# A decoder layer on one core: first-stage expert gathers split in two, four more picks in that stage, three pair buffers in the second

## The chip, the cores and the metric

The kernel runs on one core of a Trainium2 chip. The metric is the device time of one execution in microseconds (us). Engines: PE (TensorE, matmul), DVE (VectorE), ACT (ScalarE), POOL (GpSimd), SP (SyncE, which here only issues DMAs).

## What is computed

One layer of a decoder: attention and a spatial gating unit beside each other, then PEER (retrieval over 128 x 128 experts, each with one row of `u` and one of `v`), then a gated projection and a norm. 512 tokens, width 2048, float32. The change is all in PEER:

```
def peer(a, w_q, k1, k2, u_exp, v_exp):
    q = (a @ w_q).reshape(B, S, PEER_HEADS, PEER_QDIM)
    ...
    top, sel = lax.top_k(cand, PEER_TOPK)
    experts = jnp.take_along_axis(cand_idx, sel, axis=-1)
    gates = jax.nn.softmax(top, axis=-1)
    ...
        u_sel = jnp.take(u_exp, e_c, axis=0)
        h = jnp.einsum('bthkd,btd->bthk', u_sel, a_c, preferred_element_type=jnp.float32)
        w = (g_c * jax.nn.gelu(h)).astype(a_c.dtype)
        v_sel = jnp.take(v_exp, e_c, axis=0)
        return jnp.einsum('bthk,bthkd->btd', w, v_sel)
```

With 8 heads and 16 experts each, every token has 128 experts.

## The kernel before, in words

**Two ways for PEER.** For the first 344 tokens (`TD`) the kernel works densely: it multiplies with all 16384 rows of `u`, weighs the results with a sparse matrix of gates, and multiplies with all rows of `v`. For the last 128 tokens and 40 more it gathers the rows of the chosen experts. A *pick* is one gather of a `u` row and a `v` row for each of the 128 partitions: 128 picks for the last 128 tokens and 43 (`B_PICKS`, `idx_b`) for the 40 tokens, 171 in all (`PICKS`).

**The first stage** (here also: u stage) streams `peer_u` in 128 chunks, one PE slot each: `tile()` makes 16 x 3 = 48 matmuls of 344 columns (each product as three: high x high, high x low, low x high). The first 32 chunks lie between the routing steps of the heads; from chunk 36 to 118 the picks are spread over the slots. For each slot, SP loads 1 MB (`raw`), ACT rounds it (`wH`, line 656), DVE takes the rest (`wL`, line 1110), one slot ahead of PE. DVE scales the finished chunk (`scale_chunk`, 1534), ACT applies the gelu and stores it into `pair` in HBM.

**The second stage** (v stage) streams `peer_v` in 128 slots of 48 matmuls. Each slot also readies one chunk of `pair` for later: SP loads pre-activations and gates together (`pair_in`, 348 KB, `load_chunk`, 435), POOL multiplies them (`apply_gates`, 609), ACT rounds (`weight_hi`, 912) and DVE takes the rest (`weight_lo`, 1644). Eight chunks make a group, for which PE waits.

**A pick** has these steps. POOL issues the gather. DVE makes the dot product (`dot`, 1604, line 1617). ACT makes the gelu and the weight (`weigh_pick`, 923). DVE adds the weighed `v` row (`add_row`, 1619, line 1629 or 1634). The order of DVE's work is written out by hand: step `o` stands for the dot (even) or the add (odd) of pick `o // 2`, and `u_step(c)` and `v_step(g, q)` say between which slots the steps stand:

```
    return (min(max(c, FIRST_PICK), LAST_PICK) - FIRST_PICK) * 2 * (U_PICKS - LATE) // (LAST_PICK - FIRST_PICK)
```

`U_PICKS` picks belong to the first stage, `LATE` = 4 of them to its last 8 slots; the others to the second. `FIRST_PICK` is 36, `LAST_PICK` 118. In a slot DVE does: scale the last chunk, one step, `wL` for the next slot, another step where there is one. It waits in this order, so a late row holds up `wL`.

**POOL's queue** is also written by hand. The sparse matrix of gates is built by indirect DMAs that add one column of 128 gates into `pair` (`add_gates`, line 565): 384 in all, the first 156 before the first pick (`ADDS_FIRST`), the others four after each gather (614 to 619). A gather of the first stage (`gather`, 583) fetches rows of 16 KB, `u` and `v` side by side (`uv_rows`), into one of three buffers (`rows`), and waits until the pick that had the buffer is added (`pick_done`). In the second stage `gather_u` (597) and `gather_v` (605) fetch rows of 8 KB apart; the first waits for the dot of the buffer's last pick alone.

Of the kernel before, what the change touches and what calls it, by code (L numbers as in the profile page):

```python
# [27 lines left out]
HEADS = 8  # L28
# [4 lines left out]
TOPK = 16  # L33
KEYS = 128
# [18 lines left out]
FIRST_PICK, LAST_PICK = ROUTE_U + 4, KEYS - GROUP - 2  # L53
U_PICKS, LATE = 64, 4
TAIL = 6
# [120 lines left out]
def trunk_layer(nc, a, stream, out, pair_dram):  # L176
# [8 lines left out]
    def at(name, shape, dt, offset):  # L185
        return nc.alloc_sbuf_tensor_at(name, [P] + shape, dt, offset=base + offset)
# [114 lines left out]
    with ctx:  # L301
        ps = ctx.enter_context(nc.psum_tensor("ps", [P, 8, 512], F))

        def sem(name):
            return ctx.enter_context(nc.semaphore(name))
# [29 lines left out]
        pre_stored = [sem(f"pre_stored{i}") for i in range(2)]  # L335
        pair_loaded = [sem(f"pair_loaded{i}") for i in range(2)]
        g_scaled = sem("g_scaled")
# [10 lines left out]
        row_landed = [sem(f"row_landed{i}") for i in range(6)]  # L348
        v_row_landed = [sem(f"v_row_landed{i}") for i in range(3)]
        dot_done, dot_gelu, pick_weighed, pick_done = sem("dot_done"), sem("dot_gelu"), sem("pick_weighed"), sem("pick_done")  # L350
# [41 lines left out]
        def _(sp):  # L392
# [41 lines left out]

            def load_chunk(c, b):

                if isinstance(c, int):
                    sp.wait_ge(pre_stored[b], (c - b) * 8 + 16)
                if not (isinstance(c, int) and c < 2):
                    sp.wait_ge(act_wlo, c - 1)  # L440
                sp.dma_start(pair_in[b][:, :], pair_rows[:, c, 0:PW + TD]).then_inc(pair_loaded[b], 16)

            for c in range(KEYS - GROUP, KEYS):
                load(nu + c, stream["pu"][c, :, :], c % 2)
                if c == KEYS - GROUP:
# [3 lines left out]
                load_chunk(c - KEYS + GROUP, c % 2)  # L449

# [6 lines left out]
            def load_late_chunk(v):  # L457

                if v == GROUP:
                    for b in range(2):  # L460
                        sp.wait_ge(pre_stored[b], 8 * KEYS)
                load_chunk(GROUP + v, v % 2)

# [34 lines left out]
        def _(pool):  # L498
# [102 lines left out]
            def gather_v(j):  # L601

                if ROW_USED[j] >= 0:
                    pool.wait_ge(pick_done, ROW_USED[j] + 1)
                pool.indirect_dma_start(  # L605
                    out=rows[ROW_AT[j]][:, 1, :], out_offset=None, in_=a["v_rows"],
                    in_offset=bass.IndirectOffsetOnAxis(ap=ids_of(j), axis=0)).then_inc(v_row_landed[ROW_AT[j] - 3], 16)

            def apply_gates(c, b):

                pool.wait_ge(pair_loaded[b], (c - b) * 8 + 16)
                nc.gpsimd.tensor_tensor(pre_in[b], pre_in[b], gate_in[b], ALU.mult).then_inc(act_gated, 1)  # L612

            for j in range(U_PICKS - LATE + 1):
                gather(j)
                if j >= 1:
                    for n in range(added, min(added + 4, HEADS * NTD * TOPK)):
                        add_gates(n)
                        added = n + 1
            assert added == HEADS * NTD * TOPK  # L620
            for c in range(GROUP):
                apply_gates(c, c % 2)
                if c % 2 == 0 and U_PICKS - LATE + 1 + c // 2 < U_PICKS:
                    gather(U_PICKS - LATE + 1 + c // 2)
            for j in range(U_PICKS, U_PICKS + 2):
                gather_u(j)
                gather_v(j)
            for g in range(NGROUPS - 1):
                for q in range(GROUP):
                    apply_gates(GROUP * (g + 1) + q, q % 2)  # L630
# [12 lines left out]
        def _(act):  # L643
# [348 lines left out]
            def v_beat(g, q, b, m, i, tail=False):  # L992
# [3 lines left out]
                if isinstance(g, int) and (g, q) == (0, 0):  # L996
# [101 lines left out]
        def _(dve):  # L1098
# [554 lines left out]
            for c in range(ROUTE_U + 2, KEYS):  # L1653
# [654 lines left out]
```

## Time and profile before

| | us |
|---|---|
| median of 3 runs | 2978.49 (2977.01 to 2980.55) |
| the profiled execution's own time | 2979.05 |
| its span in the trace | 2977.3 |
| PE busy | 2923.9 |
| DVE busy | 2259.8 |
| ACT busy | 1268.4 |
| POOL busy | 1440.4 |

An engine's busy time is the union of its instructions; neighbouring matmuls overlap in it, so that a short stop of PE shows less idle time than it costs. On POOL an indirect DMA counts as busy for as long as POOL writes its descriptors; the transfer goes on after that.

### The profile page before, as it was taken

The numbers are of one execution on the slowest core, as the hardware profiler recorded it, in microseconds if no ns is written. First come the engines' busy times: TensorE is split into PE (matmuls) and PEld (weight loads), VectorE is DVE, ScalarE is ACT, GpSimd is POOL, SyncE is SP. The second block draws the span as 40 slices with busy tenths as digits, with TensorE's granted clock in tenths as the row PEclk, the third lists the DMA queues.
The fourth block names the chain that finished last, engine by engine and source line by source line (L and its number), as shares of the span: only waits on it lengthen the run. The fifth ranks groups of instructions, "written<-read, shape, count | busy, mean of one in ns | idle before, by whom it ended". The sixth has DMA issues, their size and how long they took to land.

```text
span 2977.3 us, 43219 instructions
## 1 busy us (share of the span) xinstructions
PE 2923.9 (98%) x16888; PEld 2739.3 (92%) x16888; DVE 2259.8 (76%) x2836; ACT 1268.4 (43%) x1898; POOL 1440.4 (48%) x859
## 2 busy tenths in 40 slices
PE   9999999999999999999999999999999999999998
PEld 7888668889999999999999999999999999999787
DVE  5466664578888877877787769888888889998545
ACT  5224541333333433333333344555555555566522
POOL 1012000008888778888888235443445778772000
PEclk9999999999999999999999999999999999999999
DMA  8469422235555599999999889999999999998222
GB/s 299 169 238 331 142 85 99 99 110 128 139 125 130 140 343 358 373 361 358 372 341 361 320 350 408 411 417 418 415 417 415 417 413 416 417 395 314 92 93 98
DMA packets 195807, 843.09 MB, mean 283 GB/s; under 512 B 66780, under 2 KB 87276, under 8 KB 116556
## 3 DMA queue, kind: packets, MB, share of 16 engines
q0 software_dynamic: 104592, 413.77, 37.9%
q1 hardware_dynamic: 72336, 404.83, 36.0%
q10 hardware_dynamic: 18732, 22.59, 2.2%
q8 instruction: 85, 1.39, 0.2%
q14 instruction: 62, 0.51, 0.0%
HBM read 768.01 MB, written 73.06 MB: 282 GB/s over the span
## 4 chain that ended last, share of the span: by engine, by line
PE 66%; DVE 13%; DMA 11%; POOL 5%; issue 3%; ACT 2%; SPq 0%; DVEq 0%; ACTq 0%; POOLq 0%
PE ps L1838 21%; PE ps L1836 21%; PE ps L1837 21%; DMA pair_in<-pair 7%; DVE wL L1110 4%; DVE rows L1617 3%; POOL pair_in L612 2%; DVE hT L1629 2%; POOL rows L597 1%; POOL rows L605 1%; DMA rows<-u_rows,idx_s 1%; DVE b_acc L1634 1%; ACT wH L656 1%; DMA rows<-v_rows,idx_b 1%; DMA raw<-s_v 1%
## 5 line engine op out<-in xcount | busy, mean ns | idle before, releaser
L1836 PE MATMUL ps<-aH,wH 128*128 128x344 f32 (+2 forms) x3088 | 1057.4, 342 | 6.3 <-DVE wL L1110 6.3
L1838 PE MATMUL ps<-aH,wL 128*128 128x344 f32 (+2 forms) x3088 | 1055.4, 342 | 0.0
L1837 PE MATMUL ps<-aL,wH 128*128 128x344 f32 (+2 forms) x3088 | 1047.1, 339 | 0.0
L565 POOL DMA_INDIRECT pair<-gates_r,idx_d x384 | 740.5, 1928 | 376.7 <-DVE gates_r L1525 242.5
L1110 DVE TENSOR_TENSOR wL<-raw,wH 128x2048 fp32r<-128x2048 f32 x333 | 778.1, 2337 | 183.2 <-ACT wH L656 180.8
L656 ACT ACTIVATE wH<-raw 128x2048 fp32r<-128x2048 f32 x333 | 636.3, 1911 | 591.5 <-PE ps L1838 538.6
L1836 PE MATMUL ps<-actH,wH 128*128 128x344 f32 x2048 | 656.7, 321 | 14.3 <-DVE wL L1110 13.8
L1838 PE MATMUL ps<-actH,wL 128*128 128x344 f32 x2048 | 656.1, 320 | 0.0
L1837 PE MATMUL ps<-actL,wH 128*128 128x344 f32 x2048 | 651.6, 318 | 0.0
L1836 PEld LDWEIGHTS ps<-aH,wH 128*128 128x128 f32 x3088 | 578.5, 187 | 47.1 <-DVE wL L1110 5.8
L1837 PEld LDWEIGHTS ps<-aL,wH 128*128 128x128 f32 x3088 | 580.6, 188 | 38.8 <-issue 1.0
L1838 PEld LDWEIGHTS ps<-aH,wL 128*128 128x128 f32 x3088 | 579.9, 188 | 38.2
L1836 PEld LDWEIGHTS ps<-actH,wH 128*128 128x128 f32 x2048 | 383.7, 187 | 21.9 <-DVE wL L1110 20.9
L1837 PEld LDWEIGHTS ps<-actL,wH 128*128 128x128 f32 x2048 | 384.9, 188 | 0.0
L1838 PEld LDWEIGHTS ps<-actH,wL 128*128 128x128 f32 x2048 | 384.1, 188 | 0.0
L612 POOL TENSOR_TENSOR pair_in<-pair_in 128x344 f32<-128x344 f32 x128 | 194.2, 1518 | 316.2 <-DMA pair_in<-pair 315.6
L1629 DVE SCALAR_TENSOR_TENSOR hT<-rows,pick_w,hT 128x2048 f32<-128x2048 f32 x128 | 305.6, 2387 | 5.4 <-issue 2.1
L1617 DVE SCALAR_TENSOR_TENSOR rows<-rows,ps 128x2048 f32<-128x2048 f32 x128 | 291.8, 2280 | 6.7 <-DMA rows<-uv_rows,idx_s 5.5
L1534 DVE TENSOR_TENSOR ut<-ps,rstd 128x344 f32<-128x344 f32 x128 | 66.0, 516 | 154.4 <-PE ps L1838 135.5
L597 POOL DMA_INDIRECT rows<-u_rows,idx_s x64 | 109.6, 1713 | 70.9 <-DVE rows L1617 48.0
L931 ACT ACTIVATE dots<-dots 128x1 f32<-128x1 f32 x128 | 25.7, 201 | 271.9 <-DVE rows L1617 262.2
L1646 DVE TENSOR_TENSOR actL<-pair_in,actH 128x344 fp32r<-128x344 f32 x128 | 67.2, 525 | 95.4 <-ACT actH L914 85.9
(288 smaller groups left out, 2626.7 us busy)
## 6 DMA issues: line engine op xcount, KB each, us to landing
raw<-s_pu SPq DMA_DIRECT2D x128, 1024.0 KB
raw<-s_pv SPq DMA_DIRECT2D x128, 1024.0 KB
pair<-zeros POOLq DMA_DIRECT2D x44, 1024.0 KB, 8.7
pair_in<-pair SPq DMA_DIRECT2D x128, 348.0 KB
pair<-ut ACTq DMA_DIRECT2D x128, 172.0 KB
raw<-s_out SPq DMA_DIRECT2D x16, 1024.0 KB
raw<-s_pq SPq DMA_DIRECT2D x16, 1024.0 KB
raw<-s_gate SPq DMA_DIRECT2D x16, 1024.0 KB
```

What stands on the lines that cost most here:

```text
L565: pool.indirect_dma_start(out=gates_flat, out_offset=bass.IndirectOffsetOnAxis(ap=idx_d[0:m, t, c:c + 1], axis=0), in_=gates_r[0:m, t, c:c ...
L597: pool.indirect_dma_start(out=rows[ROW_AT[j]][:, 0, :], out_offset=None, in_=a["u_rows"], in_offset=bass.IndirectOffsetOnAxis(ap=ids_of(j) ...
L612: nc.gpsimd.tensor_tensor(pre_in[b], pre_in[b], gate_in[b], ALU.mult).then_inc(act_gated, 1)
L656: A(wH[parity][:, :], raw[at_n][:, :], ACT.Copy).then_inc(hi_ready, 1)
L1110: V.tensor_tensor(wL[parity][:, :], src[:, :], wH[parity][:, :].bitcast(F), ALU.subtract).then_inc(lo_ready, 1)
L1534: V.tensor_tensor(ut[b][:, :], ps[:, 6 + b, 0:TD], rstd[:, 0:TD], ALU.mult).then_inc(chunk_scaled, 1)
L1617: V.scalar_tensor_tensor(r3, r3, 1.0, act_of, ALU.mult, ALU.mult, accum_out=d).then_inc(dot_done, 1)
L1629: V.scalar_tensor_tensor(hT[:, :, TA:T], v3, pick_w[:, i:i + 1], hT[:, :, TA:T], ALU.mult, ALU.add).then_inc(pick_done, 1)
L1646: V.tensor_tensor(actL[b][:, j, 0:TD], src, actH[b][:, j, 0:TD].bitcast(F), ALU.subtract).then_inc(act_wlo, 1)
L1836: mm(out, wh, xh, start=start, stop=False, skip_group_check=skip_group_check)
L1837: mm(out, wh, xl, start=False, stop=False, skip_group_check=skip_group_check)
L1838: return mm(out, wl, xh, start=False, stop=stop, skip_group_check=skip_group_check)
```

## The change

1. Each gather of the first stage becomes a `gather_u` and a `gather_v` with rows of 8 KB, with semaphores of their own; of the four `add_gates` of a pick, two stand behind each. `gather` and the array `uv_rows` go.
2. `U_PICKS` is 68 instead of 64: four picks move from the second stage into the first.
3. `pair_in` has three buffers in the second stage (chunk `c` from 8 on uses buffer `(c - 8) % 3`); a load waits for the chunk that last used its buffer, and stands one slot earlier in SP's queue.
4. In a slot of the second stage ACT rounds the chunk (`weight_hi`) before it weighs a pick instead of after.

```diff
-U_PICKS, LATE = 64, 4
+U_PICKS, LATE = 68, 4
...
+def pair_at(c):
+
+    return c % 2 if c < GROUP else (c - GROUP) % 3
...
-    pair_in = [at(f"pair_in{i}", [PW + TD], F, C0 + 4 * KB * i) for i in range(2)]
+    pair_in = [at(f"pair_in{i}", [PW + TD], F, C0 + o) for i, o in enumerate((0, 4 * KB, 7 * KB))]
...
-            def load_chunk(c, b):
-
-                if isinstance(c, int):
-                    sp.wait_ge(pre_stored[b], (c - b) * 8 + 16)
-                if not (isinstance(c, int) and c < 2):
-                    sp.wait_ge(act_wlo, c - 1)
+            def load_chunk(c):
+
+                b = pair_at(c)
+                sp.wait_ge(pre_stored[c % 2], (c - c % 2) * 8 + 16)
...
+                if PAIR_PREV[c] >= 0:
+                    sp.wait_ge(act_wlo, PAIR_PREV[c] + 1)
...
+            load_late_chunk(3)
             for v in range(3, KEYS - GROUP):
-                load_late_chunk(v)
+                if v + 1 < KEYS - GROUP:
+                    load_late_chunk(v + 1)
...
-            def gather(j):
-
-                if ROW_USED[j] >= 0:
-                    pool.wait_ge(pick_done, ROW_USED[j] + 1)
-                pool.indirect_dma_start(
-                    out=rows[ROW_AT[j]][:, :, :].rearrange("p a d -> p (a d)"), out_offset=None, in_=a["uv_rows"],
-                    in_offset=bass.IndirectOffsetOnAxis(ap=ids_of(j), axis=0)).then_inc(row_landed[ROW_AT[j]], 16)
...
             for j in range(U_PICKS - LATE + 1):
-                gather(j)
+                gather_u(j)
                 if j >= 1:
-                    for n in range(added, min(added + 4, HEADS * NTD * TOPK)):
+                    for n in range(added, min(added + 2, HEADS * NTD * TOPK)):
+                        add_gates(n)
+                        added = n + 1
+                gather_v(j)
+                if j >= 1:
+                    for n in range(added, min(added + 2, HEADS * NTD * TOPK)):
                         add_gates(n)
                         added = n + 1
...
                 if not tail:
+                    c = GROUP * (g + 1) + q
+                    weight_hi(c, q, 1 - b, pre_in[pair_at(c)])
                     for o in range(v_step(g, q), v_step(g, q + 1)):
                         if o % 2 == 0:
                             weigh_pick(o // 2)
-                    weight_hi(GROUP * (g + 1) + q, q, 1 - b, pre_in[q % 2])
...
-                if j >= U_PICKS:
-                    dve.wait_ge(v_row_landed[ROW_AT[j] - 3], 16 * ROW_TURN[j])
+                dve.wait_ge(v_row_landed[ROW_AT[j]], 16 * ROW_TURN[j])
```

The order of POOL's instructions where the picks of the first stage begin (`pair` from `gates_r` is an added column of gates, `rows` a gather; the text behind a row says what it waits for). Before:

```order
L583 DMA rows_86<-uv_rows,idx_s 128x4096 [waits a_tok_ready]
L583 DMA rows_87<-uv_rows,idx_s 128x4096
L565 DMA pair<-gates_r,idx_d 11534336x1 x4
L583 DMA rows_88<-uv_rows,idx_s 128x4096
L565 DMA pair<-gates_r,idx_d 11534336x1 x4
L583 DMA rows_86<-uv_rows,idx_s 128x4096 [waits pick_done]
```

And in the changed kernel, from the same place:

```order
L602 DMA rows_86<-u_rows,idx_s 128x2048 [waits a_tok_ready]
L610 DMA rows_86<-v_rows,idx_s 128x2048
L602 DMA rows_87<-u_rows,idx_s 128x2048
L578 DMA pair<-gates_r,idx_d 11534336x1 x2
L610 DMA rows_87<-v_rows,idx_s 128x2048
L578 DMA pair<-gates_r,idx_d 11534336x1 x2
L602 DMA rows_88<-u_rows,idx_s 128x2048
L578 DMA pair<-gates_r,idx_d 11534336x1 x2
```

Where POOL had one gather and four adds for a pick, it has two gathers and four adds.

ACT's order in a slot of the second stage (`actH` from `pair_in` is `weight_hi`, `dots` and `pick_w` are `weigh_pick`). Before:

```order
L656 ACTIVATE wH_71<-raw_67 128x2048 [waits tile_done,raw_loaded0]
L983 ACTIVATE hT<-ps 128x344 [waits h_acc,tile_done]
L973 ACTIVATE ps<-hT 128x344 [waits h_acc]
L931 ACTIVATE dots<-dots 128x1 [waits dot_done]
L935 ACTIVATE pick_w<-dots,gates_r 128x1 [waits dot_gelu]
L914 ACTIVATE actH_82<-pair_in_138 128x344 [waits act_gated]
```

And in the changed kernel:

```order
L668 ACTIVATE wH_71<-raw_67 128x2048 [waits tile_done,raw_loaded0]
L995 ACTIVATE hT<-ps 128x344 [waits h_acc,tile_done]
L985 ACTIVATE ps<-hT 128x344 [waits h_acc]
L926 ACTIVATE actH_82<-pair_in_139 128x344 [waits act_gated]
L943 ACTIVATE dots<-dots 128x1 [waits dot_done]
L947 ACTIVATE pick_w<-dots,gates_r 128x1 [waits dot_gelu]
```

The chunk's rounding stands ahead of the pick's gelu, and the buffers go round by three (137, 138, 139).

## Rows read from the trace of the kernel before

**Rows 1.** The page: span, busy time by engine, granted PE clock in 40 slices

```profile
span 2977.3 us, 43219 instructions
...
PE 2923.9 (98%) x16888; PEld 2739.3 (92%) x16888; DVE 2259.8 (76%) x2836; ACT 1268.4 (43%) x1898; POOL 1440.4 (48%) x859
PEclk9999999999999999999999999999999999999999
```

**Rows 2.** Windows of the first stage's picks and of the second stage: busy of each engine

```profile
core 0: us, PE busy (x) PEld busy (x) DVE busy (x) ACT busy (x) POOL busy (x), PEclk, DMA share, GB/s
1065.90:1761.00 695.10, 694.33 (x4401) 694.04 (x4401) 539.30 (x383) 245.08 (x320) 511.65 (x294) 1.00 0.98 355
1761.00:2754.00 993.00, 978.68 (x6177) 970.72 (x6176) 877.38 (x610) 552.30 (x977) 556.12 (x334) 1.00 1.00 406
```

**Rows 3.** Windows of 100 us inside the first and inside the second stage

```profile
1200.00:1300.00 100.00, 100.00 (x636) 100.00 (x635) 79.01 (x58) 35.27 (x47) 84.21 (x49) 1.00 1.00 360
2300.00:2400.00 100.00, 98.51 (x624) 98.09 (x623) 89.32 (x60) 56.64 (x100) 71.72 (x35) 1.00 1.02 417
```

**Rows 4.** Groups by line on POOL, 1100 to 1650 us: xcount | busy us, mean ns | idle before

```profile
L565 POOL DMA_INDIRECT pair<-gates_r,idx_d x210 | 393.3, 1873 | 73.1 <-issue 63.4 <-DMA pair<-gates_r,idx_d 9.7
L583 POOL DMA_INDIRECT rows<-uv_rows,idx_s x53 | 67.7, 1277 | 18.0 <-issue 15.5 <-DVE hT L1629 2.5
```

**Rows 5.** Timeline of POOL at the first pick and at the last adds of gates

```profile
1052.55 1.00 POOL L583 DMA_INDIRECT rows<-uv_rows,idx_s  x1 [13.09 <-DVE ps L1600]
...
1649.63 1.42 POOL L565 DMA_INDIRECT pair<-gates_r,idx_d  x1 [0.30 <-issue]
1651.36 2.51 POOL L565 DMA_INDIRECT pair<-gates_r,idx_d  x1 [0.30 <-issue]
1654.17 1.96 POOL L565 DMA_INDIRECT pair<-gates_r,idx_d  x1 [0.30 <-issue]
1656.43 0.99 POOL L583 DMA_INDIRECT rows<-uv_rows,idx_s  x1 [0.30 <-issue]
1657.73 0.97 POOL L583 DMA_INDIRECT rows<-uv_rows,idx_s  x1 [0.30 <-issue]
1685.33 0.94 POOL L583 DMA_INDIRECT rows<-uv_rows,idx_s  x1 [26.63 <-DVE hT L1629]
```

**Rows 6.** Waits of DVE for rows of picks, 1040 to 1770 us

```profile
DVE rows L1617 <- DMA rows<-uv_rows,idx_s: 5.5, 5, 1.8
```

**Rows 7.** Timeline of POOL and of DVE where an add of gates took long

```profile
1321.03 1.54 POOL L565 DMA_INDIRECT pair<-gates_r,idx_d  x1 [0.30 <-issue]
1322.87 3.24 POOL L565 DMA_INDIRECT pair<-gates_r,idx_d  x1 [0.30 <-issue]
...
1322.35 2.34 DVE L1629 SCALAR_TENSOR_TENSOR hT<-rows,pick_w,hT 128x2048 f32<-128x2048 f32 x1
1324.61 2.29 DVE L1110 TENSOR_TENSOR wL<-raw,wH 128x2048 fp32r<-128x2048 f32 x1
1326.82 2.28 DVE L1617 SCALAR_TENSOR_TENSOR rows<-rows,ps 128x2048 f32<-128x2048 f32 x1
```

**Rows 8.** Groups by line on POOL, 1770 to 2300 us, then 2300 to 2700 us

```profile
L605 POOL DMA_INDIRECT rows<-v_rows,idx_s x56 | 63.1, 1127 | 24.2 <-DVE hT L1629 14.2 <-issue 6.2
...
L605 POOL DMA_INDIRECT rows<-v_rows,idx_b x42 | 102.2, 2433 | 12.4 <-issue 7.5 <-DVE b_acc L1634 3.4
L597 POOL DMA_INDIRECT rows<-u_rows,idx_b x42 | 84.3, 2007 | 12.4 <-DVE rows L1617 4.9 <-issue 4.6
```

**Rows 9.** First matmul of each product in the second stage, 1761 to 2754 us

```profile
L1836 PE MATMUL ps<-actH,wH 128*128 128x344 f32 x2048 | 656.7, 321 | 14.3 <-DVE wL L1110 13.8
```

**Rows 10.** Waits for chunks, 1850 to 2300 us, then 2300 to 2700 us

```profile
POOL pair_in L612 <- DMA pair_in<-pair: 217.0, 53, 6.3
...
ACT actH L914 <- POOL pair_in L612: 70.6, 22, 4.1
...
POOL pair_in L612 <- DMA pair_in<-pair: 68.3, 30, 5.1
ACT actH L914 <- POOL pair_in L612: 64.7, 31, 4.1
```

More of the change, by code:

```diff
@@ L133, in raw_at @@
     return (v - 2) % 4 if 4 <= v < KEYS - GROUP else n % 2
+def pair_at(c):
+    return c % 2 if c < GROUP else (c - GROUP) % 3
+PAIR_PREV, PAIR_LANDED = [], []
+for _c in range(KEYS):
+    _same = [j for j in range(_c) if pair_at(j) == pair_at(_c)]
+    PAIR_PREV.append(_same[-1] if _same else -1)
+    PAIR_LANDED.append(16 * (1 + len(_same)))
 RAW_PREV, RAW_LANDED = [], []
@@ L335, in trunk_layer @@
         pre_stored = [sem(f"pre_stored{i}") for i in range(2)]
-        pair_loaded = [sem(f"pair_loaded{i}") for i in range(2)]
+        pair_loaded = [sem(f"pair_loaded{i}") for i in range(3)]
         g_scaled = sem("g_scaled")
@@ L348, in trunk_layer @@
         row_landed = [sem(f"row_landed{i}") for i in range(6)]
-        v_row_landed = [sem(f"v_row_landed{i}") for i in range(3)]
+        v_row_landed = [sem(f"v_row_landed{i}") for i in range(6)]
         dot_done, dot_gelu, pick_weighed, pick_done = sem("dot_done"), sem("dot_gelu"), sem("pick_weighed"), sem("pick_done")
@@ L433, in _ @@
             pair_rows = pair_dram.rearrange("(p c) s t -> p c (s t)", c=KEYS)
-            def load_chunk(c, b):
-                if isinstance(c, int):
-                    sp.wait_ge(pre_stored[b], (c - b) * 8 + 16)
-                if not (isinstance(c, int) and c < 2):
-                    sp.wait_ge(act_wlo, c - 1)
+            def load_chunk(c):
+                b = pair_at(c)
+                sp.wait_ge(pre_stored[c % 2], (c - c % 2) * 8 + 16)
+                if b == 2 and PAIR_PREV[c] < 0:
+                    for i in range(2):
+                        sp.wait_ge(pre_stored[i], 8 * KEYS)
+                if PAIR_PREV[c] >= 0:
+                    sp.wait_ge(act_wlo, PAIR_PREV[c] + 1)
                 sp.dma_start(pair_in[b][:, :], pair_rows[:, c, 0:PW + TD]).then_inc(pair_loaded[b], 16)
@@ L448, in _ @@
                     sp.wait_ge(b_loaded, 32 * SETS)
-                load_chunk(c - KEYS + GROUP, c % 2)
+                load_chunk(c - KEYS + GROUP)
             def load_value(v):
@@ L457, in load_late_chunk @@
             def load_late_chunk(v):
[L459 to L462, printed above, removed]
+                load_chunk(GROUP + v)
             for v in range(3):
@@ L606, in gather_v, with apply_gates @@
                     out=rows[ROW_AT[j]][:, 1, :], out_offset=None, in_=a["v_rows"],
-                    in_offset=bass.IndirectOffsetOnAxis(ap=ids_of(j), axis=0)).then_inc(v_row_landed[ROW_AT[j] - 3], 16)
-            def apply_gates(c, b):
-                pool.wait_ge(pair_loaded[b], (c - b) * 8 + 16)
+                    in_offset=bass.IndirectOffsetOnAxis(ap=ids_of(j), axis=0)).then_inc(v_row_landed[ROW_AT[j]], 16)
+            def apply_gates(c):
+                b = pair_at(c)
+                pool.wait_ge(pair_loaded[b], PAIR_LANDED[c])
                 nc.gpsimd.tensor_tensor(pre_in[b], pre_in[b], gate_in[b], ALU.mult).then_inc(act_gated, 1)
             for j in range(U_PICKS - LATE + 1):
-                gather(j)
+                gather_u(j)
                 if j >= 1:
-                    for n in range(added, min(added + 4, HEADS * NTD * TOPK)):
+                    for n in range(added, min(added + 2, HEADS * NTD * TOPK)):
[4 more added lines that the diff above has]
+                    for n in range(added, min(added + 2, HEADS * NTD * TOPK)):
                         add_gates(n)
@@ L621, in _ @@
             for c in range(GROUP):
-                apply_gates(c, c % 2)
+                apply_gates(c)
                 if c % 2 == 0 and U_PICKS - LATE + 1 + c // 2 < U_PICKS:
-                    gather(U_PICKS - LATE + 1 + c // 2)
+                    gather_u(U_PICKS - LATE + 1 + c // 2)
+                    gather_v(U_PICKS - LATE + 1 + c // 2)
             for j in range(U_PICKS, U_PICKS + 2):
@@ L629, in _ @@
                 for q in range(GROUP):
-                    apply_gates(GROUP * (g + 1) + q, q % 2)
+                    apply_gates(GROUP * (g + 1) + q)
                     for o in range(v_step(g, q), v_step(g, q + 1)):
@@ L959, in _ @@
                 u_beat(c, c % 2, nu + c, 0)
-                weight_hi(c - KEYS + GROUP, c - KEYS + GROUP, 0, pre_in[c % 2])
+                weight_hi(c - KEYS + GROUP, c - KEYS + GROUP, 0, pre_in[pair_at(c - KEYS + GROUP)])
                 for o in range(u_step(c), u_step(c + 1)):
@@ L1662, in _ @@
                 if c >= KEYS - GROUP:
-                    weight_lo(c - KEYS + GROUP, c - KEYS + GROUP, 0, pre_in[c % 2])
+                    weight_lo(c - KEYS + GROUP, c - KEYS + GROUP, 0, pre_in[pair_at(c - KEYS + GROUP)])
                 if late_dot:
@@ L1679, in v_end @@
                     accumulate(2 * q, CUM[m + q - 1] + 4 * GROUP * i + 1)
-                weight_lo(c, q, 1 - b, pre_in[q % 2])
+                weight_lo(c, q, 1 - b, pre_in[pair_at(c)])
             scale_chunk(KEYS - 1, 1, CUM[nu + KEYS - 1])
@@ L2276 @@
         "s_pv": v["peer_v"][0].reshape(KEYS, NGROUPS, GROUP, GROUP, WIDE).transpose(1, 3, 0, 2, 4).reshape(KEYS, P, 2048),
-        "uv_rows": np.concatenate([v["peer_u"][0], v["peer_v"][0]], axis=1),
         "u_rows": v["peer_u"][0],
```

## The prediction

> **What bounds the kernel now.** I read the page first: of a span of 2977.3 us PE is busy 2923.9, at full clock (the level of 2.4 GHz) throughout [rows 1]. So nothing that the change does can save more than PE's stops in the stages it touches, and it costs what it makes PE wait.
>
> The windows give those stops [rows 2]. In the first stage's stretch PE starts 4401 matmuls in 695.1 us, 0.1579 us each, and is idle under 1 us: there is nothing to win there. In the second stage it starts 6177 in 993.0 us; at 0.1579 each that is 975.6, so 17.4 us is all that better supply could give. The group of PE's first matmuls agrees: 14.3 us idle, 13.8 of them behind `wL` of DVE [rows 9].
>
> Next comes what stands close behind PE in the first stage. DVE is busy 79% in a window of 100 us there [rows 3]. POOL is the one to look at: its groups from 1100 to 1650 us show 393.3 us of adds of gates and 67.7 us of gathers, and 91.1 us of "idle" [rows 4]. Of that idle, 78.9 us are the 0.3 us between two of its instructions ("issue"), 9.7 us are waits for its own adds, and only 2.5 us are waits for a free buffer. In 550 us POOL stands free for 2.5. It ends its last add at 1656 us and first waits for something long (26.63 us) at 1685 [rows 5]. DVE already waited five times for a row, 5.5 us in all [rows 6]. POOL's queue is thus as full as PE's.
>
> **The cadence.** A slot is 48 matmuls, 48 x 100/636 = 7.55 us [rows 3]. `u_step` lays 60 picks over 82 slots: one each 82/60 x 7.55 = 10.32 us. POOL needs for one pick four adds and a gather, 4 x (1.873 + 0.30) + (1.277 + 0.30) = 8.69 + 1.58 = 10.27 us [rows 4]. They just match.
>
> **First edit, gathers in two.** The order of POOL shows one more indirect DMA for every pick, as the diff says. No row shows the time of an 8 KB gather among the adds; the nearest are gathers of 16 KB there, 1.277 us in the mean and 0.94 to 1.00 at the shortest [rows 4, 5], and those of 8 KB in the second stage, 1.127 us in its earlier part and 2.0 to 2.4 in its later [rows 8]. Half the bytes are not half the time: POOL pays for issuing. I take 1.277 + 0.30 = 1.58, so POOL now needs 11.85 us for a pick.
>
> **Second edit, four more picks.** 64 picks over the same 82 slots: one each 82/64 x 7.55 = 9.67 us. The deficit is 11.85 - 9.67 = 2.18 us for a pick. It lasts while there are adds to do: 384 - 156 = 228, four at each pick, 57 picks. 57 x 2.18 = 124 us. DVE's order is fixed, so a late row holds `wL` of the next slot, and PE, which has no idle time in this stage, gives all of it to the end. POOL's head start is none, since its buffers were hardly ever full.
>
> Two things make it less. POOL's instruction is held while DVE runs certain of its own: an add that took 3.24 us instead of 1.54 began at 1322.87, and ended some 1.4 us after `add_row` (1322.35 + 2.34) had [rows 7]. The mean of 1.873 has 0.33 of this over 1.54, the gather's 1.277 some 0.28 over 1.00. With PE and DVE slowed to POOL's pace, `add_row` and `wL` fill 5.3 us of 11.85 instead of 5.5 of 10.32 (2.34 + 1.28 or 1.37 x 2.29), so I shrink the excess by 16%: 0.05 for each of 6 instructions, 0.3 a pick, 17 us. And a first transfer of 1 MB lands earlier than one of 2 MB, by 1.05 MB at 360 GB/s, 2.9 us, once. That leaves 104; between 124 and 104 I take **+110 us**.
>
> The Trainium skill (SBUF — State Buffer, section "A bandwidth-pool intuition that's wrong") says that GpSimd cannot write a DMA's descriptors until DVE releases the port that they share, and gives 3100 ns in place of 620 for such a case. The row of 3.24 us agrees in kind; if every added gather cost that page's 3.1 us instead of 1.58, the deficit would be 87 us larger.
>
> Ends of this term: were every instruction as short as an undisturbed one, 4 x (1.54 + 0.30) + 2 x (1.00 + 0.30) = 9.96 us, 0.29 x 57 = +17 us [rows 5, 7]. Were both gathers as the slowest group, 2.43 + 0.30 [rows 8], 2 x 1.15 x 57 = 131 more, +241. The mean of 53 gathers under the same DVE is nearer than either.
>
> After pick 57 POOL has no adds and catches up in a few us; pick 57 now stands in slot 109, and the chunks' loads, which wait for all adds, in slot 120, eleven slots or 83 us later, so I cost the rest of the stage at nothing. Its cover is POOL's and SP's idle time there, of which the wait of 26.63 us is an instance [rows 5].
>
> **Second stage.** 103 picks instead of 107 stand in it: DVE is freed of 4 x (2.28 + 2.34) = 18 us of 877 [rows 2, 7], and 8.4 MB less are moved, 20 us at 417 GB/s [rows 3] in a stage whose DMA share is 1.00 [rows 2]. The third buffer and the earlier load act on POOL's waits for chunks, 217.0 and 68.3 us, and so on ACT's, 70.6 and 64.7 [rows 10]. All this only reaches PE through `wL`, so the gain lies between 0 and 17.4 us. With `weight_hi` first, a late chunk now holds a pick's weight and with it `add_row` and `wL`; what that could cost no row tells, and I bound it by the stage's present stops once more, 14.3 us. I take **-12 us**: fewer steps hit PE's own cause, a `wL` behind a step.
>
> **Sum.** 2979.05 (profiled execution) + 110 - 12 = 3077.1. The median of the runs lies 0.56 lower, at 2978.49, so 3076.5 us.
>
> **Rivals.**
> - *POOL fits after all* (faster). If the changed phase of its work against DVE's spares it the collisions, it needs by its shortest rows 4 x (1.42 + 0.30) + 2 x (0.94 + 0.30) = 9.36 us [rows 5]. The point is 9.67 us a pick; under it the first stage stays as it is and the second gives 12: 2966.5. Against it: the mean of 210 adds is 1.873, and even at 1.54 each it fails. Chance 0.07.
> - *The transfers bind, not POOL.* The first stage has a DMA share of 1.00 at 360 GB/s [rows 3]. If that is its limit and POOL's time gives way, 8.4 MB more cost 23 us there: 2978.5 + 23 - 12 = 2989.5. Against it: PE lost nothing in it so far, the second stage moves 417 GB/s at the same share, and the adds' length goes with DVE's instructions. Chance 0.05. The Trainium skill (DMA: Bandwidth & Descriptors, "Specifications") puts HBM's limit for a core at about 358 GB/s, which is this rival's rule; the second stage's 417 disagrees with it.
> - *Collisions grow.* POOL, now always late, falls into step with DVE as in the later second stage, and both gathers cost 2.73: 3076.5 + 131 = 3207.5. For it: [rows 8]. Against: there POOL has 8 KB gathers in a different order of DVE's work. Chance 0.05.
> - *Nothing to be seen*, by half of the first: 0.03.
>
> **Numbers.** The forecast has 0.80. The range leaves out the rivals at 2966.5, 2989.5 and 3207.5 and the outer parts of the forecast's own. Its low end goes two thirds of the way from +110 to +17, which is +48, with all of the 17.4 won: 3009. Its high end goes half of the way from +110 to +241, +175, with nothing won: 3154. About 0.2% is what a measurement of this kernel can tell from no change. Faster by more: 0.07; within: 0.03; slower: 0.90.
>
> **What would show it.** Right: the last add near 1656 + 91 + what it waits, about 1740 us; DVE's dots waiting for rows some 50 times, near 90 us in all, where it was 5.5; PE idle behind `wL` by near 100 us between 1100 and 1750; the stretch from the first pick to the second stage about 805 us instead of 695; POOL without any wait for a buffer in it; a second stage of about 981 us. Wrong: adds at 1.55 us and a first stage as long as before; or a first stage longer while POOL shows waits (then it is the transfers); or a second stage over 993 us.

## The result, and the profile after

| | before | changed |
|---|---|---|
| median, us | 2979.52 (4 runs) | 3100.95 (3099.46 to 3103.39, 4 runs) |
| the profiled execution's span, us | 2977.3 | 3097.7 |

The ratio is 1.0399 (95% interval 1.0381 to 1.0418): slower by 121 us.

The page of the changed kernel, against [rows 1]; of part 2 the slices of PE, of POOL and of the granted PE clock:

```profile
span 3097.7 us, 43283 instructions
...
PE 2962.5 (96%) x16888; PEld 2774.5 (90%) x16888; DVE 2315.2 (75%) x2836; ACT 1272.8 (41%) x1898; POOL 1497.7 (48%) x923
...
PE   9999999999999998888798899999999999999998
...
POOL 1012000028888688888888823544444666663000
PEclk9999999999999999989998999999999999999999
...
PE 68%; POOL 18%; DVE 5%; issue 5%; DMA 3%; ACT 1%; SPq 0%; ACTq 0%; DVEq 0%; POOLq 0%
```

The same rows of the kernel before that [rows 1] leaves out:

```profile
PE   9999999999999999999999999999999999999998
...
PE 66%; DVE 13%; DMA 11%; POOL 5%; issue 3%; ACT 2%; SPq 0%; DVEq 0%; ACTq 0%; POOLq 0%
```

The loss stands in one place. PE, with a 9 in every slice of the middle before, has 8s and a 7 from the 16th on; the granted clock, full before, has two 8s. And in the chain of what ended last (the last row, each engine's share of it) POOL's part rose from 5 to 18%, while those of DVE and of the DMAs fell.

The windows of the two stages and of 100 us in each, against [rows 2, 3]:

```profile
1065.90:1897.00 831.10, 736.16 (x4406) 726.18 (x4405) 558.55 (x395) 248.25 (x328) 629.03 (x365) 0.94 0.90 308
1897.00:2874.40 977.40, 973.57 (x6178) 972.24 (x6176) 914.36 (x598) 553.09 (x969) 500.26 (x326) 1.00 0.99 404
...
1200.00:1300.00 100.00, 79.44 (x469) 77.73 (x467) 61.23 (x44) 26.54 (x35) 85.68 (x48) 0.94 0.88 289
2300.00:2400.00 100.00, 100.00 (x636) 100.00 (x635) 91.55 (x57) 54.98 (x96) 44.93 (x33) 1.00 1.01 415
```

The first stage's stretch takes 831.1 us instead of 695.1 for the same matmuls (4401 and 4406 of them recorded), the second 977.4 instead of 993.0. +136.0 and -15.6: that is the whole difference of the spans, 120.4 us. In the window of 100 us in the first stage DVE fell from 79 to 61% and the DMA share from 1.00 to 0.88, while POOL went from 84 to 86%. Of the three, POOL alone had no time to lose.

In the changed kernel's lines, 578 is `add_gates`, 602 `gather_u`, 610 `gather_v`, 618 `apply_gates`, 1630 the dot, 1641 and 1646 `add_row`, 1123 `wL`, 1848 to 1850 the matmuls. POOL's groups, 1100 to 1700 us (columns as in [rows 4]), and then its timeline at the last adds of gates:

```profile
L578 POOL DMA_INDIRECT pair<-gates_r,idx_d x195 | 382.7, 1962 | 65.4 <-issue 59.2 <-DMA pair<-gates_r,idx_d 6.2
L602 POOL DMA_INDIRECT rows<-u_rows,idx_s x48 | 70.2, 1463 | 14.6 <-issue 13.1 <-DVE rows L1630 1.5
L610 POOL DMA_INDIRECT rows<-v_rows,idx_s x49 | 56.6, 1155 | 14.9 <-issue 14.9
```

```profile
1760.51 1.45 POOL L578 DMA_INDIRECT pair<-gates_r,idx_d  x1 [0.30 <-issue]
1762.27 1.42 POOL L578 DMA_INDIRECT pair<-gates_r,idx_d  x1 [0.31 <-issue]
1764.00 0.99 POOL L602 DMA_INDIRECT rows<-u_rows,idx_s  x1 [0.30 <-issue]
```

POOL's idle time is "issue", 0.3 us each, 6.2 us of waits for its own adds, and 1.5 us of waits for a buffer. An add takes 1.962 us (it was 1.873), the two gathers 1.463 and 1.155 us. So a pick costs POOL 4 x 2.262 + 1.763 + 1.455 = 12.27 us. The last add ends at 1763.7 us instead of 1656.1.

Who waits for it, 1040 to 1900 us (before: [rows 6], and the last line here, from 1040 to 1770 us of the kernel before):

```profile
DVE rows L1630 <- DMA rows<-u_rows,idx_s: 110.2, 33, 5.5
DVE hT L1641 <- issue: 97.5, 32, 5.6
...
DVE hT L1641 <- DMA rows<-v_rows,idx_s: 6.6, 3, 2.8
...
PE ps L1848 <- DVE wL L1123: 94.9, 34, 6.1
...
PE ps L1836 <- DVE wL L1110: 0.8, 1, 0.8
```

DVE waits 33 times for a `u` row and 32 times before an add of a `v` row ("issue" is a wait whose releaser the profile does not name; it stands at the same instruction as the three waits for `v_rows`). PE then waits 94.9 us behind `wL`, which stands behind those steps in DVE's order. That is less than the 136 us by which the stage grew; the rest is time in which PE ran at the lower clock (last section).

In the second stage, PE's first matmuls (against [rows 9]) and waits from 1990 to 2440 us (against [rows 10]):

```profile
L1848 PE MATMUL ps<-actH,wH 128*128 128x344 f32 x2048 | 656.5, 321 | 3.8 <-DVE wL L1123 3.8
...
POOL rows L610 <- DVE hT L1641: 129.9, 43, 5.0
...
POOL pair_in L618 <- DMA pair_in<-pair: 9.9, 7, 2.9
```

PE's idle time fell from 14.3 to 3.8 us. POOL waited 217.0 us for chunks in the stretch shown before; now it waits for buffers of picks instead.

### The profile page after: what moved, and what is told of

It reads as the page before. It is cut to its first block, busy times and chain, and to the rows that moved or that the text cites. A ratio compares the mean times of both kernels' runs of the same rounds, so it can differ in the third digit from the quotient of the medians.

```text
span 3097.7 us, 43283 instructions
## 1 busy us (share of the span) xinstructions
PE 2962.5 (96%) x16888; PEld 2774.5 (90%) x16888; DVE 2315.2 (75%) x2836; ACT 1272.8 (41%) x1898; POOL 1497.7 (48%) x923
## 3 DMA queue, kind: packets, MB, share of 16 engines
q8 instruction: 85, 1.39, 0.2%
## 4 chain that ended last, share of the span: by engine, by line
PE 68%; POOL 18%; DVE 5%; issue 5%; DMA 3%; ACT 1%; SPq 0%; ACTq 0%; DVEq 0%; POOLq 0%
PE ps L1850 22%; PE ps L1848 22%; PE ps L1849 22%; POOL pair L578 13%; POOL rows L602 2%; POOL rows L610 2%; DVE wL L1123 1%; DMA rows<-u_rows,idx_s 1%; DVE hT L1641 1%; DMA rows<-v_rows,idx_s 1%; ACT wH L668 1%; PE ps L2046 1%; DVE rows L1630 1%; PE ps L2102 0%; PE ps L2023 0%
## 5 line engine op out<-in xcount | busy, mean ns | idle before, releaser
L1848 PE MATMUL ps<-aH,wH 128*128 128x344 f32 (+2 forms) x3088 | 1076.8, 349 | 100.5 <-DVE wL L1123 100.5
L1849 PE MATMUL ps<-aL,wH 128*128 128x344 f32 (+2 forms) x3088 | 1065.2, 345 | 0.0
L1848 PEld LDWEIGHTS ps<-aH,wH 128*128 128x128 f32 x3088 | 593.3, 192 | 151.2 <-DVE wL L1123 109.6
L1849 PEld LDWEIGHTS ps<-aL,wH 128*128 128x128 f32 x3088 | 594.8, 193 | 38.5 <-issue 1.0
L1850 PEld LDWEIGHTS ps<-aH,wL 128*128 128x128 f32 x3088 | 593.5, 192 | 38.3
L1641 DVE SCALAR_TENSOR_TENSOR hT<-rows,pick_w,hT 128x2048 f32<-128x2048 f32 x128 | 330.2, 2580 | 110.0 <-issue 99.1
L1630 DVE SCALAR_TENSOR_TENSOR rows<-rows,ps 128x2048 f32<-128x2048 f32 x128 | 291.9, 2281 | 112.7 <-DMA rows<-u_rows,idx_s 110.2
L602 POOL DMA_INDIRECT rows<-u_rows,idx_s x128 | 178.9, 1398 | 234.0 <-DVE rows L1630 188.7
L610 POOL DMA_INDIRECT rows<-v_rows,idx_s x128 | 185.8, 1452 | 192.7 <-DVE hT L1641 170.9
L618 POOL TENSOR_TENSOR pair_in<-pair_in 128x344 f32<-128x344 f32 x128 | 150.7, 1178 | 44.1 <-DMA pair_in<-pair 41.7
L1646 DVE SCALAR_TENSOR_TENSOR b_acc<-rows,pick_wb,b_acc 128x2048 f32<-128x2048 f32 x42 | 132.6, 3156 | 2.7 <-ACT pick_wb L947 1.7
```

What stands on the lines that cost most here:

```text
L602: pool.indirect_dma_start(out=rows[ROW_AT[j]][:, 0, :], out_offset=None, in_=a["u_rows"], in_offset=bass.IndirectOffsetOnAxis(ap=ids_of(j) ...
L610: pool.indirect_dma_start(out=rows[ROW_AT[j]][:, 1, :], out_offset=None, in_=a["v_rows"], in_offset=bass.IndirectOffsetOnAxis(ap=ids_of(j) ...
L1630: V.scalar_tensor_tensor(r3, r3, 1.0, act_of, ALU.mult, ALU.mult, accum_out=d).then_inc(dot_done, 1)
L1641: V.scalar_tensor_tensor(hT[:, :, TA:T], v3, pick_w[:, i:i + 1], hT[:, :, TA:T], ALU.mult, ALU.add).then_inc(pick_done, 1)
L1646: V.scalar_tensor_tensor(b_acc[:, :, :], v3, pick_wb[:, i:i + 1], b_acc[:, :, :], ALU.mult, ALU.add).then_inc(pick_done, 1)
L1848: mm(out, wh, xh, start=start, stop=False, skip_group_check=skip_group_check)
```

## The experiments

Each kernel ran beside the kernel before on the same chip, where that one's median was 2981.8 to 2982.5 us; the ratios are to those runs. "Stage 1 end" is the start of the first matmul of the second stage in the PE timeline: 1761.0 us before, 1897.1 in the changed kernel. "Stage 2" is from there to the end of its last matmul: 993.0 and 977.3 us. Each is from one profile. Kernels whose second stage is the same differ in it by 1 to 2 us (before and `split_only`; `picks_only` and `picks_aligned`), and the first pick began up to 4.3 us later than before (`picks_only`), so differences of that size say nothing.

### The two halves of the first stage's edit, apart

`split_only` is the kernel before with the two gathers of 8 KB and the adds two and two (its two main lines):

```diff
-                gather(j)
+                gather_u(j)
...
+                gather_v(j)
```

> The kernel before with one edit: gathers of the first stage as two of 8 KB rows, adds two and two; 64 picks there, second stage as it was. POOL's queue (my theory): POOL needs per pick four adds and two gathers, 12.27 us by the changed kernel's profile (4 x 2.26 + 1.76 + 1.46), against 10.32 us between picks; 57 x 1.95 = 111 us, so about 3090 us, with adds of gates back to back and DVE waiting for rows. Transfers bind (rival): not a byte is added, so about 2980 us. Half and half between splitting and the added picks (a second rival, that the loss is of the four more picks alone): about 2980 us too.

Measured: 3089.79 us, ratio 1.0352 (1.0328 to 1.0376). Last add 1769.3 us, stage 1 end 1872.4, stage 2 995.0. Not one byte was added, and 111.4 of the 136 us are there, as POOL's queue gives it. The rival that the added picks do it alone is gone.

`picks_only` is the kernel before with `U_PICKS` 68:

```diff
-U_PICKS, LATE = 64, 4
+U_PICKS, LATE = 68, 4
```

> The kernel before with one edit: 68 instead of 64 picks in the first stage, gathers of 16 KB kept. POOL's queue: 10.27 us of POOL for a pick against 9.67 between picks, 57 x 0.6 = 34 us in the first stage, less some 8 us that four picks fewer give in the second: about 3005 us. Transfers bind: 8.4 MB more at 360 GB/s in the first stage, 23 us, less 8: about 2994 us, and then POOL would show waits for buffers; by POOL's queue it shows none.

Measured: 3015.64 us, ratio 1.011 (1.0088 to 1.0131). Last add 1668.7, stage 1 end 1811.4 (+50.4), stage 2 980.0 (-13.0). Both theories were too low. The last add comes only 12.6 us later than before, but the picks now stand earlier: pick 57 in slot 109 instead of 114, 5 x 7.55 = 38 us. 12.6 + 38 = 51, the lengthening measured. Of the 12.6 us, 4.3 were there at the first gather (1056.9 instead of 1052.6 us); for the rest, the 228 adds took 1.94 us in the mean instead of 1.89.

The two halves make 111.4 + 50.4 = 161.8 us, more than the 136.1 of both together: the 4.3 us are in it, and in each half alone the adds grew (by 0.09 and 0.05 us) as much as or nearly as much as in the kernel with both (0.07). The rest of the difference is not accounted for.

### Is it POOL's time or the transfers?

`short_v` is the changed kernel with 2 KB of each first-stage `v` row instead of 8:

```diff
-                    out=rows[ROW_AT[j]][:, 1, :], out_offset=None, in_=a["v_rows"],
+                    out=rows[ROW_AT[j]][:, 1, 0:D // 4] if short else rows[ROW_AT[j]][:, 1, :], out_offset=None,
+                    in_=a["v_short"] if short else a["v_rows"],
```

> The changed kernel, but from pick 3 on the v row of a first-stage pick is fetched with 2 KB instead of 8 KB; the rest of the row stays as an earlier pick left it, so this part of the sum is left out. POOL issues the same instructions, the transfers of a pick shrink from 2.1 MB to 1.3 MB. POOL's queue: nothing moves, about 3098 us, first stage about 830 us from 1066. Transfers bind: 65 x 0.79 MB less at 360 GB/s, 142 us less: about 2965 us.

Measured: 3101.61 us, ratio 1.0396 (1.0367 to 1.0426); last add 1764.3, stage 1 end 1899.4. POOL's groups from 1100 to 1700 us and the window 1200 to 1300:

```profile
L578 POOL DMA_INDIRECT pair<-gates_r,idx_d x194 | 375.6, 1936 | 65.0 <-issue 58.5 <-DMA pair<-gates_r,idx_d 6.4
L602 POOL DMA_INDIRECT rows<-u_rows,idx_s x48 | 81.0, 1687 | 14.6 <-issue 14.3 <-DVE rows L1632 0.3
L611 POOL DMA_INDIRECT rows<-v_short,idx_s x49 | 51.1, 1044 | 14.9 <-issue 14.9
...
1200.00:1300.00 100.00, 85.04 (x488) 83.61 (x489) 64.67 (x47) 27.43 (x38) 85.07 (x50) 0.91 0.77 230
```

230 GB/s instead of 289, a DMA share of 0.77 instead of 0.88, and the time is the changed kernel's. The bytes do not bind. The rows also say what POOL pays for: 1.044 us for a gather of 2 KB rows, 1.155 for one of 8 KB, 1.277 for one of 16 KB [rows 4], all of them means that hold some collisions with DVE.

This leaves the number of transfers, which `short_v` keeps. In the changed kernel, at the 33 dots for which DVE waited, the dot began 4.6 to 7.8 us after POOL's gather instruction had ended, 6.6 us in the mean of the earlier half and 6.7 in that of the later. Had the transfers piled up behind POOL, this time would have grown.

`no_adds` takes POOL's other work away (one place of the edit is shown; the kernel leaves 228 columns of gates out of the result):

```diff
-                if j >= 1:
-                    for n in range(added, min(added + 2, HEADS * NTD * TOPK)):
-                        add_gates(n)
-                        added = n + 1
                 gather_v(j)
```

> The changed kernel without the 228 adds of gates that stand among the picks (three quarters of the sparse gates of five heads are left out). Gathers of 8 KB and 68 picks stay. POOL's queue: a pick costs POOL 3.3 us against 9.67, the first stage is back at 695 us, total about 2960 us. Were it DVE or the added transfers that 68 picks overload, some of the 136 us would stay, at least the 23 us of the added bytes or DVE waiting for rows.

Measured: 2964.29 us, ratio 0.9931 (0.9904 to 0.9958). The windows of its two stages:

```profile
1066.00:1761.70 695.70, 695.70 (x4411) 695.70 (x4410) 558.33 (x395) 246.68 (x328) 277.91 (x138) 1.00 0.94 368
1761.70:2739.00 977.30, 973.28 (x6178) 971.46 (x6176) 915.06 (x598) 553.09 (x969) 501.24 (x326) 1.00 0.99 403
```

The first stage is at 695.7 us, PE without any idle time, POOL at 40%. DVE with 68 picks and the transfers with 368 GB/s have room. The run takes away the adds' small transfers along with POOL's time for them; that these did not hold the rows up is the reading just before.

### Can the four picks be had without the loss?

`joined_spread` is the changed kernel with gathers of 16 KB again and the 228 adds spread over 64 picks:

```diff
-                    for n in range(added, min(added + 2, HEADS * NTD * TOPK)):
...
+                    for n in range(added, ADDS_FIRST + (HEADS * NTD * TOPK - ADDS_FIRST) * j // (U_PICKS - LATE)):
```

> The changed kernel with gathers of 16 KB again and the 228 adds of gates spread over all 64 picks of the loop (3 or 4 at each) instead of four at each of 57; 68 picks, three pair buffers and the new rounding order kept. POOL's queue: 3.56 x 2.17 + 1.58 = 9.3 us for a pick against 9.67 between picks, so the first stage is back at about 696 us and the second keeps its 977: about 2963 us, faster than both kernels. Transfers bind: the first stage still has 8.4 MB more, 23 us: about 2986 us.

Measured: 2988.77 us, ratio 1.0014 (0.9998 to 1.0029). Stage 1 end 1787.3, 26.3 us too long; stage 2 976.5. The total is near the transfers' 2986, but `short_v` speaks against that theory, and the expectation from POOL's queue missed by 26 us. POOL's timeline at the first border between two heads, and all such waits:

```profile
1157.64 0.99 POOL L596 DMA_INDIRECT rows<-uv_rows,idx_s  x1 [0.30 <-issue]
1158.93 1.45 POOL L578 DMA_INDIRECT pair<-gates_r,idx_d  x1 [0.30 <-issue]
1172.13 1.55 POOL L578 DMA_INDIRECT pair<-gates_r,idx_d  x1 [11.74 <-DMA pair<-gates_r,idx_d]
...
POOL pair L578 <- DMA pair<-gates_r,idx_d: 37.2, 4, 11.7
```

The first add of a head waits until the adds of the head before have landed (the kernel says so in `add_gates`). Here the last of those was issued right behind a gather of 2 MB, and POOL stood 11.74 us; before, a gather lay between that add and the wait, and the longest wait was 3.6 us.

`joined_aligned` lets a head's adds end with a pick:

```diff
+            def adds_by(j):
+
+                ends = [(0, 156), (10, 192), (23, 240), (37, 288), (50, 336), (64, 384)]
+                for (j0, n0), (j1, n1) in zip(ends, ends[1:]):
+                    if j <= j1:
+                        return n0 + (n1 - n0) * (j - j0) // (j1 - j0)
```

> As joined_spread, but the adds of a head now end with a pick, so that the next head's first add, which waits for them, stands behind one more gather. In joined_spread those four waits cost POOL 37.2 us (up to 11.7 each), because the last add had just been issued behind a gather; before they cost 3.2 each. If that is the cause of its first stage being 26 us longer, the waits fall to about 13 us, the first stage to within 5 us of 695 and the whole to about 2966 us. If it is POOL's mean load (3.6 adds and a gather, 9.4 to 9.7 us against 9.67), 2985 us stays.

Measured: 2969.71 us, ratio 0.9962 (0.9949 to 0.9975). Its stages, and POOL's waits from 1050 to 1720 us:

```profile
1066.00:1761.20 695.20, 694.32 (x4401) 694.04 (x4400) 556.76 (x395) 246.73 (x328) 512.25 (x298) 1.00 0.99 367
1761.20:2738.80 977.60, 973.99 (x6178) 972.55 (x6176) 917.25 (x598) 552.99 (x969) 502.12 (x326) 1.00 1.00 404
...
POOL rows L596 <- DVE hT L1651: 48.2, 13, 16.7
...
POOL pair L578 <- DMA pair<-gates_r,idx_d: 11.6, 4, 4.6
```

The four waits cost 11.6 us, POOL has 48.2 us of slack (waits for a buffer), the first stage is at 695.2 and the second at 977.6 us. This kernel is faster than both, than the kernel before by 0.4%.

`split_aligned` has the same spread with gathers of 8 KB, two adds behind the `u` row and the rest behind the `v` row:

```diff
-                    for n in range(added, min(added + 2, HEADS * NTD * TOPK)):
+                    for n in range(added, min(added + 2, adds_by(j))):
...
                 gather_v(j)
...
-                    for n in range(added, min(added + 2, HEADS * NTD * TOPK)):
+                    for n in range(added, adds_by(j)):
```

> The changed kernel, gathers of 8 KB kept, with the adds of gates spread over 64 picks as in joined_aligned. By POOL's queue its work from the first pick to the last add stays the same, so the last add still ends near 1764 us; but what must not be late is now pick 64 and not 57, whose slot is 7 x 9.67 = 68 us later. So the first stage is 136 - 68 = 68 us longer than before instead of 136, in all about 3032 us. If the lag were a matter of the adds' placement alone, as joined_aligned might suggest, it would be near 2970 us.

Measured: 3071.93 us, ratio 1.0287 (1.0242 to 1.0333); last add 1808.4, stage 1 end 1876.8. The expectation missed by 40 us: I had left out that up to pick 64 POOL also issues seven more picks' gathers, 7 x 3.2 = 23 us, and the gathers of `v` took 1.46 us in the mean. It also looked at the last add alone, while each of the 64 picks was late by itself: 3.56 adds and two gathers are 3.56 x 2.24 + 1.71 + 1.76 = 11.46 us by this run's means, 1.79 more than the 9.67 between picks, and 64 x 1.79 = 115 us against 115.8 measured. Placement alone does not save the split.

### The second stage's edits

`second_only` is the changed kernel with 64 picks and gathers of 16 KB again, and `order_only` the kernel before with ACT's new order:

```diff
-U_PICKS, LATE = 68, 4
+U_PICKS, LATE = 64, 4
...
-                gather_u(j)
+                gather(j)
```

```diff
+                    weight_hi(GROUP * (g + 1) + q, q, 1 - b, pre_in[q % 2])
                     for o in range(v_step(g, q), v_step(g, q + 1)):
                         if o % 2 == 0:
                             weigh_pick(o // 2)
-                    weight_hi(GROUP * (g + 1) + q, q, 1 - b, pre_in[q % 2])
```

> The kernel before with the second stage's edits alone: three pair buffers and the chunk's rounding ahead of the pick's gelu; 64 picks and gathers of 16 KB. The second stage of the changed kernel was 15.7 us shorter. If the supply of chunks is what held PE there, most of it stays with 107 picks: about 2967 us, second stage about 981. If it was the four picks fewer, nothing: 2979 us. The first stage stays at 695 us by both.

> The kernel before with ACT rounding the chunk ahead of the pick's gelu, nothing else; both second-stage edits together brought the stage from 993.0 to 989.0 us. If the third buffer did that, the stage stays at 993 or gets longer, since ACT now waits for late chunks with a pick's weight behind; if the order did it, about 990 us.

Measured: `second_only` 2977.93 us, ratio 0.9982 (0.9964 to 1.0001), stage 2 989.0 us; `order_only` 2983.86 us in its one run, stage 2 997.6 us. So with 107 picks the two edits are worth some 4 us in that stage, which the times cannot tell from nothing, and not the 15.7.

Two more take one or both edits out of `joined_aligned`, with 68 picks and the spread adds. `picks_aligned` has neither: it is the kernel before with `U_PICKS` 68 and `adds_by`. `buffers_aligned` has the third buffer and the old order:

```diff
-                    weight_hi(c, q, 1 - b, pre_in[pair_at(c)])
                     for o in range(v_step(g, q), v_step(g, q + 1)):
                         if o % 2 == 0:
                             weigh_pick(o // 2)
+                    weight_hi(c, q, 1 - b, pre_in[pair_at(c)])
```

> joined_aligned without the second stage's edits: two pair buffers and the old rounding order, 68 picks, gathers of 16 KB, adds spread. With four picks more in the first stage the second took 980.0 us in picks_only and 977.6 with the edits. If those two are worth what these spans say, this one has a first stage of 695 us and a second of about 980, about 2.5 us over joined_aligned. If the third buffer is needed for the gain, the second stage is back near 990.

> joined_aligned with the old rounding order (pick's gelu first), three pair buffers kept. order_only made the second stage 997.6 instead of 993.0 us in one look; if the new order costs 4 us by itself, this one is up to 4 us faster than joined_aligned; if the order doesn't matter once chunks come early, both are the same, near 977 us in the second stage.

Measured: `picks_aligned` 2969.56 us, ratio 0.9942 (0.9917 to 0.9966), stage 2 981.2; `buffers_aligned` 2978.96, ratio 0.9979 (0.9964 to 0.9994), stage 2 987.5. Four picks fewer give the gain without any of the two edits. With three buffers and the old order the stage is 10 us longer than with the new one (and its first stage ended at 1765.6); so the order is needed once the third buffer is there. Together they give 3.6 us in the stage and nothing in the time: 2969.71 us with both, 2969.56 with neither. Why the old order costs more with three buffers than with two was not followed up.

## Why the prediction was right

The mechanism was the forecast's: POOL's issuing was full, the change made its work for a pick longer and the time between picks shorter, and PE waited. The cadence orders every kernel. "POOL, a pick" is measured: from the start of the second pick's gather to the end of the last add, its waits for its own adds included and those for buffers taken off, divided by the picks in between; "longer by" is how much later than before stage 1 ended, less how much later its picks began.

| kernel | POOL, a pick | between picks | picks | sum | stage 1 longer by |
|---|---|---|---|---|---|
| before | 10.51 | 10.32 | 57 | 11 | 0 |
| split_only | 12.51 | 10.32 | 57 | 125 | 112 |
| picks_only | 10.72 | 9.67 | 57 | 59 | 46 |
| changed | 12.40 | 9.67 | 57 | 155 | 136 |
| short_v | 12.39 | 9.67 | 57 | 155 | 137 |
| joined_spread | 10.15 | 9.67 | 64 | 30 | 23 |
| split_aligned | 11.70 | 9.67 | 64 | 129 | 113 |
| joined_aligned | 9.48 | 9.67 | 64 | none | 0 |
| picks_aligned | 9.52 | 9.67 | 64 | none | 0 |
| buffers_aligned | 9.80 | 9.67 | 64 | 8 | 2 |
| second_only | 10.33 | 10.32 | 57 | 1 | 0 |
| order_only | 10.34 | 10.32 | 57 | 1 | 0 |

Kernels with the same first stage differ in POOL's time for a pick: 10.33 to 10.51 us (before, `second_only`, `order_only`) and 9.48 to 9.80 (the three aligned ones with gathers of 16 KB), so a sum is good to some 10 to 20 us. Where there is a lengthening, it stays 6 to 19 us below the sum. The likely reason is POOL's head start, which the prediction took for none: in the kernel before, pick 10's gather ended at 1149.9 us and its dot began at 1170.9, while a row of 16 KB that DVE waited for was used 9.7 and 9.4 us after its gather (picks 49 and 57). POOL was some 11 us ahead, and in the kernel before its shortfall of 11 us cost nothing.

- **The cadence** (10.27 us of POOL against 10.32 between picks, then 11.85 against 9.67) was the right reading, and the 2.18 us over 57 picks, 124 us, the right kind of sum. POOL's price was 12.27 us by the means of its groups.
- **The step that was mis-sized** is the one that took 17 us off because PE and DVE run slower and collisions would get rarer. They did get rarer, but each cost more. Counted in the trace, 119 of the 228 adds among the picks began before while `add_row` or `wL` ran, and took 2.23 us in the mean; in the changed kernel 91 did, and took 2.61. The others took 1.51 us in both. So the price was 12.27 instead of the forecast's 11.55: the 17 us should not have come off, and (12.27 - 11.85) x 57 = 24 us more came on. The timeline shows two such adds (changed kernel, POOL, then DVE):

```profile
1333.85 3.02 POOL L578 DMA_INDIRECT pair<-gates_r,idx_d  x1 [0.30 <-issue]
...
1340.70 3.21 POOL L578 DMA_INDIRECT pair<-gates_r,idx_d  x1 [0.30 <-issue]
...
1333.11 2.35 DVE L1641 SCALAR_TENSOR_TENSOR hT<-rows,pick_w,hT 128x2048 f32<-128x2048 f32 x1 [3.18 <-issue]
1335.37 2.28 DVE L1123 TENSOR_TENSOR wL<-raw,wH 128x2048 fp32r<-128x2048 f32 x1
...
1338.00 2.28 DVE L1630 SCALAR_TENSOR_TENSOR rows<-rows,ps 128x2048 f32<-128x2048 f32 x1
...
1340.20 2.29 DVE L1123 TENSOR_TENSOR wL<-raw,wH 128x2048 fp32r<-128x2048 f32 x1
```

- **The head start**, put at none, hid the other way: 124 + 24 is 148, and 136 was measured. 3 us had been taken off for the earlier landing; the other 9 are within what POOL was ahead. That the two errors partly cancel is luck.
- **The rest of the first stage at nothing**: right. After its last add POOL issues the coming gathers back to back, and the chunks came in time.
- **The second stage**, forecast -12, measured -15.7. Right in size, and the runs say whose it is: 13.0 us come with four picks fewer (`picks_only`), and what the other two edits add to that, some 3 us in the stage, the times do not show.
- **The signs.** The last add came at 1763.7 us (1740 was named), PE's waits were 94.9 us (near 100), POOL's for a buffer 1.5 us (none). DVE waited for a `u` row 33 times and 110.2 us (some 50 and 90), and in addition some 104 us before adds: with the `v` row issued two adds later than the `u` row, it waits twice for a pick, which the prediction did not name. Nor did it name the fall of PE's clock.
- **Rivals.** That POOL fits after all fell with the 12.27 us; that the bytes bind fell with `short_v`; growing collisions were real, but a fifth of that rival's 131 us. The +110 was short by 26 us, the second stage's -12 by 4, the other way: the forecast was 3076.5, the time 3100.95.

## What to carry to other kernels

Add up an engine's issuing time for each period of the steady state, its fixed gap between instructions (0.3 us on POOL here) included, and set it against the period: POOL at "84% busy" was full. An edit that adds instructions to such a queue costs them nearly in full, however few bytes they carry; and a change that shortens the period costs the same way. Where work of different urgency shares the queue, spread the work that isn't urgent to the end of the stage, and put what must have landed ahead of large transfers.

## What was not expected of the hardware

PE's granted clock fell in the lengthened stage. Three windows around the first fall, and the PE timeline there:

```profile
1135.00:1142.00 7.00, 5.02 (x32) 4.73 (x30) 3.65 (x3) 1.44 (x4) 5.48 (x6) 1.00 0.91 296
1142.00:1149.00 7.00, 6.04 (x21) 6.04 (x22) 7.00 (x5) 1.50 (x2) 6.08 (x4) 0.51 0.96 315
1149.00:1156.00 7.00, 7.00 (x47) 7.00 (x46) 1.51 (x3) 2.61 (x4) 5.78 (x5) 1.00 1.07 366
...
1139.70 0.32 PE L1850 MATMUL ps<-aH,wL 128*128 128x344 f32 x1
1142.96 0.66 PE L1848 MATMUL ps<-aH,wH 128*128 128x344 f32 x1 [2.94 <-DVE wL L1123]
1143.41 0.49 PE L1849 MATMUL ps<-aL,wH 128*128 128x344 f32 x1
1143.70 0.49 PE L1850 MATMUL ps<-aH,wL 128*128 128x344 f32 x1
```

After 2.94 us without a matmul the clock is at 0.51 in the next window, so nearly all of it at the level of 1.2 GHz, and matmuls start 0.29 us apart instead of 0.16; in the window after it is full again. In the stage the mean is 0.94; the trace's record of the clock has 95.6 of the 831.1 us at the lower level. Half of that, 48 us, and the 94.9 us of waits make 143, near the 136 by which the stage grew. The same holds in the other kernels: `split_only` 79.5 us of waits and 64.9 at the lower level, 112 (112 measured); `split_aligned` 75.7 and 75.1, 113 (113).

This is where PE spent the time and not why it lost it. POOL waited 1.5 us in 600 for a buffer and so hardly ever for PE or DVE, and the table of cadences fits kernels with such stretches (changed, split_only, 0.94 and 0.96) and without (joined_aligned, 1.00) alike: a PE that waits for POOL anyway has the slack to run slow in. What the clock would cost by itself was not measured.

A wait for one's own small transfer grew with what was queued just ahead of it: 11.74 us where the last add stood right behind a gather of 2 MB (`joined_spread`), at most 3.6 us in the kernel before and 4.6 in `joined_aligned`, where it did not.
